# Weight remainders of the delta layer: the engine that computes them and their place in VectorE's order

## The reference, cut to what matters

```
hn   = rms_norm(x, g)
proj = hn @ w_in                        # q, k, v, gate of 8 heads, 128 wide each
q, k, v = silu(short_conv(...)), q and k L2-normalised
o    = delta rule, forward and backward in time, per head (chunks; a triangular inverse per chunk)
o    = rms_norm per head * silu(gate);  x = x + o @ w_out
```

## Time and profile before

| | |
|---|---|
| median of 3 runs | 1344.1 us (1343.12 to 1345.96) |
| the profiled execution, own time | 1348.23 us |
| its span, first to last instruction | 1346.5 us |
| mean granted TensorE clock | 0.982 of full |
| delta layer's projections | from about 520 to 1190 us of the span |

### The profile page before, as it was taken

One profiled execution on the slowest core, in us unless ns is written; L12 is line 12 of the kernel. 1 busy time (PEld: TensorE's weight loads), 2 busy tenths in 40 slices (PEclk: granted clock), 3 DMA queues, 4 the chain that ended last, 5 costly groups with the idle time before them and its releaser, 6 DMA issues.

```text
span 1346.5 us, 23647 instructions
## 1 busy us (share of the span) xinstructions
PE 1273.6 (95%) x8829; PEld 975.2 (72%) x8829; DVE 854.4 (63%) x2340; ACT 692.0 (51%) x1806; POOL 277.5 (21%) x188
## 2 busy tenths in 40 slices
PE   5999999999989989778999999999999999989997
PEld 4866766766666766667888888888888888865643
DVE  5334445444447655795897978879788797852343
ACT  6245465464544454525657475574856647552121
POOL 7220111020134235113104031040310403100000
PEclk9999999999989999888999999999999999999999
DMA  5110111011312132101112111120201101053111
GB/s 194 33 34 29 32 32 32 17 38 57 125 63 94 47 119 101 49 32 48 32 33 64 33 48 48 36 68 26 67 29 64 48 18 64 1 220 110 48 65 76
DMA packets 21761, 79.94 MB, mean 59 GB/s; under 512 B 3216, under 2 KB 3472, under 8 KB 20240
## 3 DMA queue, kind: packets, MB, share of 16 engines
q1 hardware_dynamic: 21648, 78.42, 17.1%
HBM read 63.66 MB, written 14.75 MB: 58 GB/s over the span
## 4 chain that ended last, share of the span: by engine, by line
PE 74%; DVE 11%; ACT 9%; issue 3%; DMA 1%; POOL 1%; SPq 0%; DVEq 0%; ACTq 0%; POOLq 0%
PE bank L1866 19%; PE bank L1766 17%; PE bank L1842 5%; PE bank L1906 4%; PE bank L1881 4%; PE bank L1793 3%; PE bank L1804 3%; PE bank L1819 3%; DVE arena L1505 3%; PE bank L1958 2%; PE bank L1965 2%; PE bank L1991 2%; PE bank L1940 2%; PE bank L1939 2%; PE bank L1951 2%
## 5 line engine op out<-in xcount | busy, mean ns | idle before, releaser
L1866 PE MATMUL bank<-hn_hi,w_hi 128*128 128x512 f32 x512 | 222.6, 435 | 0.5 <-ACT arena L1148 0.5
L1866 PE MATMUL bank<-hn_hi,w_lo 128*128 128x512 f32 x512 | 202.2, 395 | 0.0
L1866 PE MATMUL bank<-hn_lo,w_hi 128*128 128x512 f32 x512 | 201.6, 394 | 0.0
L1766 PE MATMUL bank<-hn_hi,w_hi 128*128 128x512 f32 x320 | 136.8, 428 | 0.5 <-ACT arena L1083 0.2
L1766 PE MATMUL bank<-hn_hi,w_lo 128*128 128x512 f32 x320 | 126.0, 394 | 0.0
L1766 PE MATMUL bank<-hn_lo,w_hi 128*128 128x512 f32 x320 | 125.8, 393 | 0.0
L1004 POOL TENSOR_TENSOR w_lo<-arena,w_hi 128x1024 fp32r<-128x1024 f32 x24 | 59.8, 2494 | 301.6 <-ACT w_hi L1179 301.6
L1114 ACT ACTIVATE arena<-bank 128x512 f32<-128x512 f32 x88 | 52.3, 598 | 123.8 <-PE bank L1804 123.8
L1866 PEld LDWEIGHTS bank<-hn_hi,w_lo 128*128 128x128 f32 x512 | 96.9, 189 | 21.9
L1364 DVE CUSTOM_DVE_ANT_0 arena<-bank,arena 128x384 f32<-128x384 f32 (+1 forms) x128 | 70.1, 581 | 66.1 <-issue 65.7
L1866 PEld LDWEIGHTS bank<-hn_hi,w_hi 128*128 128x128 f32 x512 | 97.8, 191 | 16.5 <-ACT arena L1148 0.7
(11 more groups left out here) (258 smaller groups left out, 2749.2 us busy)
## 6 DMA issues: line engine op xcount, KB each, us to landing
arena<-in_w SPq DMA_DIRECT2D x52, 512.0 KB, 3.5
arena<-in_x SPq DMA_DIRECT2D x16, 512.0 KB, 4.6
arena<-gc_scratch SPq DMA_DIRECT2D x8, 1024.0 KB, 4.7
x_scratch<-arena SPq DMA_DIRECT2D x13, 512.0 KB, 3.7
arena<-x_scratch SPq DMA_DIRECT2D x13, 512.0 KB, 4.0
out<-arena SPq DMA_DIRECT2D x8, 512.0 KB, 2.6
oT_scratch<-arena SPq DMA_DIRECT2D x7, 512.0 KB, 5.3
arena<-oT_scratch SPq DMA_DIRECT2D x7, 512.0 KB, 7.8
```

The costliest lines, as they stand in the source:

```text
L1766: ins = te.matmul(bank[r % 2][:], wp[:, tile % 2, k], hp[:, k, hf * HALF:(hf + 1) * HALF], start=(k == 0 and m == 0), stop=(k == KT - 1 an ...
L1866: ins = te.matmul(b[:], wp[:, t % 2, k], hp[:, k, hf * HALF:(hf + 1) * HALF], start=(k == 0 and m == 0), stop=(k == KT - 1 and m == 2))
```

## The change

`by_dve(t)` becomes `t >= 5`, so the remainders of the tiles 5 to 31 (27 of them) are all DVE's, and only 3 stay with POOL at L1004. The event `wrest` for tile t moves: it stands right behind the piece (t-1, first half, k = 6), which is the seventh piece behind the release of the place by tile t-2. The events `wrest` at the end of the recurrence are gone. DVE's waits and instruction at `wrest`, SP's wait at `ws` and PE's wait are as they were.

```diff
+        def by_dve(t):
+            return t >= 5
+
         def layer1_order():
...
                     if e[2:] == (1, KT - 1) and e[1] + 2 < NTILES:
                         ev.append(("ws", e[1] + 2))
+                    if e[2:] == (0, 6) and e[1] + 1 < NTILES and by_dve(e[1] + 1):
+                        ev.append(("wrest", e[1] + 1))
...
-                        19: sub[17:20], 20: sub[20:22], 21: sub[22:24], 22: sub[24:] + spread(h) + [("wrest", 4 * h + 4)] * (h < B_HEADS - 1)}
+                        19: sub[17:20], 20: sub[20:22], 21: sub[22:24], 22: sub[24:] + spread(h)}
...
-        def by_dve(t):
-
-            return t % 4 == 0 and t >= 8
```

## The result

| kernel | median (us) | range, runs | ratio to before, 95% interval |
|---|---|---|---|
| before, beside it | 1345.03 | 1343.12 to 1346.44, 4 | |
| after | 1368.49 | 1366.99 to 1370.34, 4 | 1.0172 [1.0158, 1.0187] |

The change makes the kernel slower by 23.5 us. Its profiled execution took 1368.51 us. In every kernel with the change the lines are two higher than before: `ktr` and `otr` transpose at L1993, `otr` is evicted at L1592, `tab1` is at L1555, SP issues tiles at L881 and ET at L886. In the other kernels they are shifted by a few more (e4's `ktr` is L1999).

A forecast was written before the change was run, and what follows sets the result against it. The prediction took PE, busy for 95% of the span, to bound the kernel. Head 0's -3.0, the stalls' 22.2 and the clock's 9.0 sum to +28.2 us on the median 1344.1, giving 1372.3 us, range 1356 to 1388.

The forecast's parts named there:

- The main term: Heads 2 to 7: ET's load, queued on SP behind a remainder, delays `ktr`; 3.7 us each, 22.2 us in all.
- The load's duration: ET's load ahead of `tab1`, running behind a weight load: 6.2 us, against 4.7 us alone.
- The clock: Half clock on PE behind each of the six `ktr` stalls: 1.5 us each, 9.0 us in all.
- Rival 1: At `ktr`, PE stalls without the clock falling: +19.2 us, so 1363.3 us; chance 0.20.
- Head 0: Tile 5's remainder no longer slows DVE's convolution taps: PE's stall 2.0 us shorter, clock 1.0 us, together -3.0 us.
- Head 1: At `tab1` of head 1 the late ET load costs 0, with no `otr` or `onorm` there.
- The other added work at 0: DVE's 21 added remainders, 25 us, ahead of `rec c` in the recurrence and ahead of `sub o`, cost PE 0.
- Rival 2: Remainders ahead of `rec c` make DVE late in the recurrence: 8 to 17 us on top, 1380 to 1389; chance 0.08.

The follow-up runs named there:

- e4: The kernel after, but at tiles 4h+1 SP, still waiting for the remainder, issues ET's load ahead of the weight load; 1354.20 us, ratio 1.0077.
- e1: The kernel after, with SP issuing the load of tile t+2 at `wrest` of tile t where DVE computes the remainder, not at `ws`; 1339.67 us.
- e3: The kernel before, with only the remainders of tiles 9, 13, ..., 29 (q tiles) moved to DVE at the new place; 1372.61 us, ratio 1.021.
- e5: The kernel before, with only tile 5's remainder moved to DVE at the new place, SP's order unchanged; 1342.59 us, ratio 0.998.
- e7: The kernel after, with four more projection pieces ahead of `ktr`, taken from four later steps of the recurrence; 1369.42 us, ratio 1.0182.

## Why the prediction was right

It said 1372.3 us, slower, in 1356 to 1388; measured were 1368.49. Step by step:

- **The main term's place and cause: right.** SP issues the tile's load and then ET's (882.04, 882.47), behind the remainder; e1, which moves SP's wait and nothing of DVE's, takes all of the loss away, and e3 shows that the six q tiles carry it.
- **The load's duration: sized too long.** "I take 1.5 us more", 6.2 us; it took 5.5 us at the median, 0.8 above the 4.7 of before. The rest of the chain came as worked out: ET's issue 4.46 us behind the end of `wqq` (4.4 in the working), the eviction 0.68 us behind `tab1`, `ktr` 0.80 us behind that. Only `ktr` itself took 0.28 us longer and not 0.1. The six waits with these halves gave 20.7 us (19.0 + 1.7) for the 22.2 predicted. One load of 7.0 us, which no row foresaw, makes the 4.40 of head 3's `ktr`; with a wait like the others there the sum would be 19.2.
- **The clock: right as a sum, in part by luck, and not in each head.** 9.0 us predicted, 8.5 measured, but in five of six heads and in two sizes: 1.3 to 1.6 us for a stretch of 3.41 us, 2.65 for the one of 6.83. Rival 1, waits without the clock, would have been 9 us less, and e4 shows that it holds for waits of up to 1.7 us. The luck: e3's six waits of the same kind had three falls, 4.7 us.
- **Head 0: the stall right** (4.36 to 2.40). For the clock it took 1.0 us; the profile after has 2.7, e5 1.2 and e1 0.6, so the size is one of the run and not of the change alone.
- **Head 1: the step that failed.** "ACT's exponential and POOL's masks shift by about as much as PE does: 0." There PE has no stall of its own, so in the profile after nothing shifted PE, and 2.0 us of the masks' delay reached it (2.28 less 0.26). In e5, with PE held up by the clock, it was 0.4. e7 made the same chain the main loss in every head.
- **The other added work at 0: right.** Heads of e1 differ from those of before by 0.1 us at most. Rival 2's mechanism exists (e3, 2.4 us in all); it shows where POOL has a remainder behind the late masks, and the change itself takes that away. DVE also got time back where POOL no longer runs beside it: 21 more remainders are 25 us, but its busy time rose by 8.6 us only (854.4 to 863.0). PE did not wait for it either way.

The terms as measured: -2.0 (head 0) + 2.0 (head 1) + 20.7 + 8.5 = 29.2 us. The profiles' difference from 597.6 to 1198.5 is 24.7. Of the 4.5 us between, before's own half clock of 6.83 us in head 0 has 2.7 (PE's starts from 618.2 to 626.1). The last 1.8 us, 0.8 of them behind head 7, are spread thin and stay open. The forecast lay 3.8 us above the measured 1368.49: the loads were taken too long by 1.5 us in sum, the half clock of head 0 gave back more than was taken, and head 1's 2.0 us were missing the other way.

## What to carry to other kernels

When one list orders all engines, an event that is moved behind an engine's work also moves every queue that waits at it: look for the transfers that stand behind that wait, and put the wait where its own transfer is issued. Then ask who reads the late data on each engine; here there were two chains, and the longer stall hid the other. An engine that sets the time and is busy for 95% of the span may still have short waits in each pass that are worth as much as a change under study: here 0.8 and 0.5 us of waiting stood for 1.9 us per head.

## What the runs showed of the hardware that was not expected

- Six waits of PE of 1.5 to 1.7 us by starts (e4) were never followed by a lower clock; waits of 2.8 to 4.4 us were in five of six cases (after), of 2.9 to 3.2 us in three of six (e3). The stall of 2.4 us in head 0 was in three of seven. Equal waits got different answers, and stretches were of 3.41, 6.83 or 10.24 us.
- A 1 MB load into ET that follows a weight load by 0.4 us takes 5.5 us, 0.8 to 0.9 more than alone or ahead of it (4.7 before, 4.6 in e4), and the weight load in front took 3.3 to 3.8 us (after), hardly more than the 3.4 to 3.5 of before. Single loads took 6.8 (e1, with no transfer ahead of it), 7.0 (after) and 8.7 us (e7).
- Where POOL and DVE met, the records fit two engines that wait for each other once, not two that both run slowly. In head 0 before, the three taps take 1.28, 3.29 and 1.28 us one by one. POOL's remainder starts 0.13 us behind the first and takes 3.40 us, 1.03 more than the 2.37 of the earlier trace rows; the second tap ends 1.08 us behind POOL's end. Step 1 of head 3 has the same 1.08 (890.13 to 891.21).
- The remainder on DVE takes 1221 ns in the new place, 1181 in the old.
